# Adding a broadcast row inside an accumulating DMA instead of on VectorE: one Trainium2 core, a hybrid LRU, attention and mixture-of-experts step

## The reference, cut to what matters

```python
def modulate(x, g, shift, scale):
    return rms_norm(x, g) * (1 + scale) + shift

x = x + g1 * merge_branches(y_rnn, y_att, gates, w_br_rnn, w_br_att, w_out)
h = modulate(x, norm_g[1], sh2, sc2)          # sh2: one row of 1024 for the prompt, one for the latents
scores = sigmoid(h @ w_router)                # 16 scores a token
# best group of four experts, the best two in it, weights from their scores
y = sum over experts e: combine[:, e] * ((silu(h @ w_gate[e]) * (h @ w_up[e])) @ w_down[e])
x = x + g2 * y
```

## Time and profile before

| | us |
|---|---|
| median of 3 runs | 1199.46 (1199.22 to 1202.29) |
| the profiled execution | 1198.25 |
| its span, first to last instruction | 1196.3 |
| TensorE busy | 1107.3 (93%) |
| VectorE busy | 909.7 (76%) |
| ScalarE busy | 678.9 (57%) |
| GpSimd busy | 256.1 (21%) |
| mean granted TensorE clock | 0.970 |

### The profile page before, as it was taken

The page is one execution under the profiler, slowest core; times in us unless marked ns, Lnnn a source line. Parts: engine busy times, 40 slices in busy tenths (PEclk is TensorE's granted clock), DMA queues, the critical chain, the costliest instruction groups (busy, mean ns, idle before and its releaser), DMA issues.

```text
span 1196.3 us, 19808 instructions
## 1 busy us (share of the span) xinstructions
PE 1107.3 (93%) x7082; PEld 1014.9 (85%) x7082; DVE 909.7 (76%) x1255; ACT 678.9 (57%) x1041; POOL 256.1 (21%) x139
## 2 busy tenths in 40 slices
PE   5999999999999999999999999995999999999950
PEld 1599999999999998899999999995788888888840
DVE  6748797978879796866556637558799998999928
ACT  3646757666666756642222212455688877877824
POOL 0132222122222122233333323201110110110011
PEclk9899999999999999999999999997999999999985
DMA  9235412212111221134444445538799999999945
GB/s 366 98 113 160 148 48 81 72 67 84 56 63 57 79 69 50 41 130 152 140 140 141 140 148 192 173 114 316 291 396 421 424 411 418 405 414 427 366 151 200
DMA packets 54569, 232.17 MB, mean 194 GB/s; under 512 B 5328, under 2 KB 22000, under 8 KB 46064
## 3 DMA queue, kind: packets, MB, share of 16 engines
q1 hardware_dynamic: 50480, 216.79, 48.2%
q0 software_dynamic: 4032, 14.68, 3.2%
HBM read 210.45 MB, written 21.00 MB: 193 GB/s over the span
## 4 chain that ended last, share of the span: by engine, by line
PE 50%; DVE 4%; ACT 1%; issue 1%; DMA 1%; POOL 0%; DVEq 0%; SPq 0%; ACTq 0%; POOLq 0%
PE PS L943 24%; PE PS L710 21%; PE PS L935 1%; PE PS L815 1%; PE PS L956 1%; PE PS L860 1%; DVE xo L1947 1%; DVE xo L1949 1%; DVE hrow L1780 0%; PE PS L906 0%; DMA G<-slot_rows,slotI 0%; DVE yo L1959 0%; DVE WgLo L1883 0%; DVE acc L1604 0%; PE PS L848 0%
## 5 line engine op out<-in xcount | busy, mean ns | idle before, releaser
L604 POOL TENSOR_TENSOR wLo<-wRaw,wHi 128x1024 fp32r<-128x1024 f32 x80 | 202.9, 2537 | 547.3 <-ACT wHi L1020 547.2
L710 PE MATMUL PS<-hHi,wHi 128*128 128x320 f32 x896 | 285.2, 318 | 4.3 <-DVE hLo L1435 1.9
L710 PE MATMUL PS<-hLo,wHi 128*128 128x320 f32 x896 | 277.4, 310 | 0.0
L710 PE MATMUL PS<-hHi,wLo 128*128 128x320 f32 x896 | 277.4, 310 | 0.0
L710 PEld LDWEIGHTS PS<-hHi,wHi 128*128 128x128 f32 x896 | 169.4, 189 | 5.6 <-issue 3.2
L710 PEld LDWEIGHTS PS<-hLo,wHi 128*128 128x128 f32 x896 | 169.1, 189 | 0.0
L710 PEld LDWEIGHTS PS<-hHi,wLo 128*128 128x128 f32 x896 | 168.8, 188 | 0.0
L1604 DVE SCALAR_TENSOR_TENSOR acc<-adaL,csil,acc 128x512 f32<-128x512 f32 x112 | 103.8, 985 | 10.3 <-DMA adaL<-in_w_ada_late 9.9
L1020 ACT ACTIVATE wHi<-wRaw 128x1024 fp32r<-128x1024 f32 x80 | 84.1, 1051 | 44.8 <-PE PS L710 44.7
L1883 DVE TENSOR_TENSOR WgLo<-Wg,WgHi 128x2048 fp32r<-128x2048 f32 x34 | 76.4, 2287 | 13.0 <-ACT WgHi L1241 12.9
L1883 DVE TENSOR_TENSOR WdLo<-Wd,WdHi 128x2048 fp32r<-128x2048 f32 x34 | 76.4, 2288 | 9.5 <-ACT WdHi L1241 9.2
(11 more groups left out here) (324 smaller groups left out, 2764.9 us busy)
## 6 DMA issues: line engine op xcount, KB each, us to landing
wRaw<-in_wtiles SPq DMA_DIRECT2D x80, 512.0 KB, 3.4
Wu<-in_experts SPq DMA_DIRECT2D x18, 2048.0 KB, 9.4
Wg<-in_experts SPq DMA_DIRECT2D x18, 2048.0 KB, 9.7
Wd<-in_experts SPq DMA_DIRECT2D x17, 2048.0 KB
adaL<-in_w_ada_late SPq DMA_DIRECT2D x32, 512.0 KB, 4.3
slot_rows<-Ys SPq DMA_DIRECT2D x18, 512.0 KB, 10.7
ada<-in_w_ada SPq DMA_DIRECT2D x8, 1024.0 KB, 17.7
slot_rows<-tab SPq DMA_DIRECT2D x10, 512.0 KB, 6.5
```

The source lines that it names most:

```text
L604: nc.gpsimd.tensor_tensor(wLo[b][:], wRaw[b][:], wHi[b][:].bitcast(F32), ALU.subtract).then_inc(w_lo, 1)
L710: r = mm(PS[:, bank, 0:HALF], w[:, k, :], x[:, k, cols], start=(k == 0 and w is wHi[b] and x is xh), stop=(k == KT - 1 and w is wLo[b]))
```

## The change: what it does

Row tiles 0 to 3 of `h2d` are filled with the shift rows ahead of time. SP issues five broadcasts instead of two: four write the shift to the rows of a tile in DRAM, the fifth fills `shb`, which is now one row of 1024. In the router stretch GpSimd issues one accumulating DMA for each of tiles 0 to 3, as soon as ScalarE has evicted the tile: it adds `hrow` to the rows in DRAM. Tile 4 is added on VectorE as before, now between the maximum over the groups and the comparison behind it, and SP writes it to DRAM. SP waits for the four accumulations before it asks for the next Wg. GpSimd's gathers and ScalarE's first down weights wait for the accumulations and for the fifth tile. On TensorE the four residual groups that stood behind the ranks stand ahead of them.

```diff
-    shb = region(x1t_at + 4 * (TT - 2) * D)("shb", [2, D])
+    shb = region(x1t_at + 4 * (TT - 1) * D)("shb", [D])
@@ SP
-        for g in range(2):
-            sp.dma_start(shb[:, g].rearrange("p (k c) -> p k c", c=P),
-                         shd.rearrange("(k g) c -> g k c", g=2)[g].unsqueeze(0).broadcast_to([P, KT, P])) \
+        for t in range(TT):
+            dst = h2d[t * P:(t + 1) * P, :] if t < TT - 1 else shb[:]
+            sp.dma_start(dst.rearrange("p (k c) -> p k c", c=P),
+                         shd.rearrange("(k g) c -> g k c", g=2)[min(t, 1)].unsqueeze(0).broadcast_to([P, KT, P])) \
                 .then_inc(h2_pre, 16)
...
-        for t in range(TT):
-            sp.wait_ge(slot_ok, t + 1)
-            sp.dma_start(h2d[t * P:(t + 1) * P, :], hrow[:, t, :]).then_inc(hrow_out, 16)
+        sp.wait_ge(slot_ok, 1)
+        sp.dma_start(h2d[(TT - 1) * P:TT * P, :], hrow[:, TT - 1, :]).then_inc(h2_pre, 16)
+        sp.wait_ge(hrow_out, 16 * (TT - 1))
         load(0, 1, 1)
@@ GpSimd
+        pool.wait_ge(h2_pre, 16 * (TT + 1))
+        for t in range(TT - 1):
+            pool.wait_ge(tr_ev, 2 * (t + 1))
+            nc.gpsimd.dma_start(h2d[t * P:(t + 1) * P, :], hrow[:, t, :], accum_op=ALU.add).then_inc(hrow_out, 16)
+
         pool.wait_ge(idx_ok, 1)
-        pool.wait_ge(hrow_out, 16 * TT)
+        pool.wait_ge(hrow_out, 16 * (TT - 1))
+        pool.wait_ge(h2_pre, 16 * (TT + 2))
@@ TensorE
         to_rows(0, xa, range(2 * TT))
+        to_rows(1, x1, range(4))
...
         x.then_inc(rk_mm, 1)
-        to_rows(1, x1, range(4))
@@ ScalarE
-        act.wait_ge(hrow_out, 16 * TT)
+        act.wait_ge(hrow_out, 16 * (TT - 1))
+        act.wait_ge(h2_pre, 16 * (TT + 2))
@@ VectorE
-        dve.wait_ge(h2_pre, 48)
-
-        def shifted(t):
-
-            dve.wait_ge(tr_ev, 2 * (t + 1))
-            v.tensor_tensor(hrow[:, t, :], hrow[:, t, :], shb[:, min(t, 1)], ALU.add).then_inc(slot_ok, 1)
-
         st(v.scalar_tensor_tensor(top2[:], in_rank[:], 1.5, sel[:], ALU.is_lt, ALU.mult))
-        shifted(0)
-        shifted(1)
...
         st(v.tensor_reduce(r5[0][:], gscore[:], AX, ALU.max))
-        shifted(2)
-        shifted(3)
+        dve.wait_ge(tr_ev, 2 * TT)
+        dve.wait_ge(h2_pre, 16 * (TT + 1))
+        v.tensor_tensor(hrow[:, TT - 1, :], hrow[:, TT - 1, :], shb[:], ALU.add).then_inc(slot_ok, 1)
...
-        shifted(4)
```

More of the change, by code:

```diff
@@ L646, in _ @@
             pool.wait_ge(ys_out[b], 16 * more + 8 * E)
-        pool.wait_ge(slot_ok, TT + 1)
+        pool.wait_ge(slot_ok, 2)
         pool.sem_inc(ticks, 1)
```

## The result

Six runs of the changed kernel took 1214.3 us in the median (1213.2 to 1219.4). The kernel before, run between them, took 1202.1 us (1199.2 to 1207.0). The ratio is 1.0108, with a 95% interval of 1.0082 to 1.0134: 1.1% slower, 12 us by the medians and 13 us by the ratio, where 5 us slower had been forecast and the range ended at 1209.5. The profiled execution took 1213.31 us, its span is 1211.1 us (before 1196.3), the mean granted clock 0.964 (before 0.970). Busy times hardly moved: TensorE 1108.3 us, VectorE 906.8, ScalarE 679.9, GpSimd 258.5. The difference lies in waits.

A forecast was written before the change was run, and what follows sets the result against it. The prediction took TensorE's always-busy expert stage as the bound, so its start, set by the first gather, passes to the end. Gather +4.0 and clock +1.0 gave +5.0 us, 1204.5 us as the median; range 1197.5 to 1209.5.

The forecast's parts named there:

- VectorE, 3.3 us earlier: Router chain on VectorE: four of five shift additions leave, so everything up to the index comes 3.3 us earlier.
- TensorE's order and SP's fill, 0 each: Residual groups move into TensorE's idle time before the ranks; SP's three more broadcasts stay within the weight tile's margin; cost 0.
- Rival 4: The fill holds up the weight tiles by more than 7.3 us: +2 to +3 us on any case; chance 0.03.
- margin of 7.3 us: Time from GpSimd finishing the next weight tile (773.7) to TensorE wanting it (781.0), set against SP's later request.
- Accumulation at twice a copy, 2.58 us a tile: DMA engines, router stretch: two operands per row, so twice a 1.29 us transfer for each accumulated tile.
- Rival 1: Accumulations at a copy's price land at 817.8; nothing is left of the gain, 1199.5 (1198 to 1201); chance 0.27.
- rival 3: Accumulations at three times a copy or worse: landed at 828, gather 836, 1209 to 1212; chance 0.12.
- The landing of the rows: DMA engines finish loads, fifth tile and four accumulations at 821.3; rows land 1.6 us later, at 822.9.
- The new wait takes the place of the one removed: GpSimd's gather waits for the accumulated rows until 822.9, though the index is ready at 818.4.
- The gather beside the load, 8.2 us: First gather, issued together with Wg's load, lands after 8.2 us instead of 5.1, at 831.1: +4.0 us.
- The clock, +1.0 us: TensorE after its idle time: first gathered tile's transposes at low clock +0.6, longer slow gate products +0.4 us.
- Rival 2: Rows' landing is no bound and the gather slips ahead of Wg: L935 at 823.8, -3.3 us, 1196.2; chance 0.12.

The follow-up runs named there:

- e1: Changed kernel, but SP asks for Wg only when the first two gathers have landed; ratio 1.0041 to the kernel before, median 1206.4 us.
- e2: Changed kernel, but SP asks for Wg without waiting for the accumulations; ratio 1.0073 to the kernel before.
- e8: Changed kernel with Wg behind the first two gathers and Wd's first load behind the first gather; ratio 1.0062 to the kernel before.
- e12: Changed kernel with GpSimd's memset of onesH split into 12 pieces; one run, profiled span 1208.2 us.
- e5: Kernel before with only TensorE's four residual groups moved ahead of the ranks; ratio 1.0008.
- e6: Kernel before with four more broadcasts of shift rows, into rows of h2d that the usual writes later cover; ratio 1.0007.
- e3: Changed kernel with plain copies from GpSimd in place of the four accumulating DMAs, tiles 0 to 3 unshifted; ratio 1.0038 to the kernel before.
- e4: Changed kernel without shift for tiles 0 to 3: no filling, no accumulation, plain writes by SP; ratio 0.9999 to the kernel before, median 1202.3 us.
- e10: Changed kernel with only tiles 0 and 1 accumulated, tiles 2 and 3 added on VectorE, Wg behind both gathers; ratio 1.0040 to the kernel before.

## Why the prediction came out right in direction and wrong in size

**VectorE, 3.3 us earlier: right.** Measured from `top` to the index: 2.75 us, and 3.1 us in e1, e2, e8 and e12. Most of the rest is ScalarE, whose evictions ended 2.3 us behind the start of `top` instead of 1.9, so that VectorE waited 1.59 us instead of 1.29.

**TensorE's order and SP's fill, 0 each: right** (e5, e6). **Rival 4 fell** with them. The prediction set its margin of 7.3 us against "a slip of 1 to 2 us"; the slip on GpSimd was 4.6 us, and the margin held.

**Accumulation at twice a copy, 2.58 us a tile: right,** 2.6 us by the queues of e3 and of the changed kernel. Rival 1 (the price of a copy) and rival 3 (three times) fell as prices. The rule quoted from the Trainium skill, Collectives: The Full Stack (Part 3, the bandwidth ceiling), that a reduce with two reads on one ring runs at half the rate of a copy, agrees with the 2.06.

**The landing of the rows: right, in part by luck.** Forecast at 822.9 with `top` at 806.84, +16.1; measured at 826.02, +16.6. By the packets' times in the trace, the engines were done with the accumulations at +16.3 and not at +14.5 (821.3), and the landing followed 0.3 us behind and not 1.6: two errors that nearly cancel. From the last issue to its landing it was 15.2 us, not the 13 forecast, and the first packet came 4.8 us behind its issue, not 2.2. The new wait takes the place of the one removed, as forecast; the index now waits 5.8 us for the gather's issue.

**The gather beside the load, 8.2 us: this is the step that failed.** It took 11.69 us, and GpSimd needed 0.85 us more from the landing to the issue, which the sum did not have. Together with the 0.55 us of the landing and 0.1 us to TensorE's start that is the 5.0 us by which L942 is later than forecast. The prediction read "5.1 us of load lie on the engines with the gather", one load. It had not followed Wu. Of ScalarE's earlier work on Wu it said "nobody waits for it so early. Cost 0, gain 0": but VectorE's low part behind it releases SP's next load of Wu, which so far had been asked for just after the gather's landing. With VectorE 2.8 us faster and the gather 2.6 us later, that load fell 0.2 us behind the gather's issue. Also, of the gathers in the earlier trace rows, which took 8.2 to 12.3 us, I took the lowest "as the load has only begun". A load that has only begun is all still ahead, so that was a reason for the upper half. e1 puts both loads behind the gathers and has 4.31 us from issue to the transposes; e3 has 8.2 us with Wg alone at the start, so one load costs what was forecast, and the rest is read as Wu's share. By the packets' times the first packet of the gather moves 4.7 us behind the issue in e3 and 4.6 us in the changed kernel: what Wu adds is the time behind that, 7.1 us instead of 3.5. (e3 has copies in place of the accumulations, so this is a comparison of two kernels, and no clean test of Wu.) The DMA queues of the changed kernel, in the first 2.1 us behind the gather's issue, in the next 2.2, and over all of the gather:

```profile
q1 hardware_dynamic: 35, 0.57, 101.0%
...
q1 hardware_dynamic: 52, 0.85, 94.1%
...
q0 software_dynamic: 157, 0.58, 12.2%
q1 hardware_dynamic: 257, 3.95, 86.0%
```

There is no packet of GpSimd's queue (q0) in the first two answers, so in the first 4.3 us; in e1, on free engines, the first moved 1.8 us behind the issue. Then the two queues share: a packet of the loads holds an engine for 0.86 x 11.7 x 16 / 257 = 0.63 us, one of the gather for 0.15 us. If the engines take turns, the ten packets (157 over 16 engines) that each has of the gather need about 7.8 us instead of 1.5, and 4.3 + 7.8 is close to the 11.69. That is an argument from these sums, in line with the rule on turns that the prediction quoted from the Trainium skill, DMA: Bandwidth & Descriptors (Queues, rings and completion order); the turns themselves I did not read from the trace.

**The clock, +1.0 us: right.** The eight transposes took 1.95 us instead of 1.11 (+0.84, forecast +0.6), and the gate products' slow start cost 0.2 us more (forecast +0.4). Stretches at the low clock move single profiles by as much elsewhere: 0.7 to 1.0 us ahead of `top`, 1.2 and 1.6 us behind the gate in e4.

**Not foreseen: 2.3 us at the end**, with an instruction load in GpSimd's wait, which e12 takes away without touching the change's work.

The sum by steps: forecast +4.0 and +1.0; measured +9.04 and +0.84, and 2.3 us at the end. With 0.7 us of low clock ahead of `top` and 1.9 us of scatter up to the projection, the two spans differ by 14.8 us, and the medians by 12.2. The runs of e1 fit this account: without the collision its gate is 2.5 us later than before and its end 2.3 us, 4.8 us together, and the ratio says 0.41%, 4.9 us. So close a match is luck, as the interval is 1.8 to 8.2 us. Rival 2 (faster by 3.3 us) needed rows landed by 818.4, 11.6 us behind `top`. e4 has them 10.8 us behind it, and a gate 3.2 us earlier did not show in twelve runs (-1.8 to +1.7 per thousand, so 2.2 us at most): that an earlier start passes through to the end was not borne out there, and the reason is open.

## What to carry to other kernels

An addition put into a DMA cost two transfers on the DMA engines here (2.6 us of all 16 for a tile, against 1.3 for a copy and 1.2 us of VectorE). Where the engines are full, or where the result is read back at once, it must be timed from issue to landing (10 to 15 us here), not by the issue (1 us). For a small urgent transfer, write down when each large load around it will be asked for after the change, those whose buffers an earlier finish of another engine frees included. Two such loads cost 7.4 us here, more than the 2.8 us that the change had won on VectorE, and two more waits in SP's order removed that.

## What the runs showed of the hardware that was not expected

- An indirect gather of 512 KB lands 4.2 us after its issue on free DMA engines (e1), after 8.2 us with one load of 2 MB just ahead (e3), and after 11.7 us with two asked for around it (the changed kernel). Its first packet moves after 1.8, 4.7 and 4.6 us.
- GpSimd's first instruction after the expert loop started 0.80 or 3.06 us after its data had landed. In all six profiles with the late start a packet of 8 KB of the kind `instruction` moves in that wait, and in none of the eight others. Splitting a memset, far ahead of it, into 12 pieces changed it from the one to the other.
- Four VectorE operations with two SBUF inputs took five times as long beside GpSimd additions (2.52 against 0.49 us). Of the first two gathers, one issued beside VectorE's work on WuLo took 1.8 to 2.9 us to issue, and otherwise 1.0 to 1.1.
- GpSimd issued its gather 0.85 us behind a DMA's landing (the changed kernel, e1, e2, e8, e10), and 0.3 us behind VectorE's index (the kernel before, e3, e4).
